# A background plan over 64 steps instead of 32, and experts added one by one instead of some in couples

## What is computed

```python
for i in range(DEPTH):                                    # 2 layers
    if i % 2 == 0: y = diff_attention(h)                  # paged K/V cache for the 8 new tokens
    else:          y = short_conv(h)                      # h @ w_in (3072 columns), width 3, @ w_out
    h = layer_norm(ALPHA * h + y)
    h = layer_norm(ALPHA * h + peer_ffn(h))
    h = h + sigmoid(h @ w_gate) * (p @ w_proj)

def peer_ffn(x):                                          # for each token
    q = (x @ w_q).reshape(8 heads, 2, 128)
    s = einsum(q, keys)                                   # 8 heads x 2 x 128 key scores
    sv, si = top_k(s, 16)
    cand = sv[0][:, None] + sv[1][None, :]                # 256 candidates of a head
    top_s, top_p = top_k(cand, 16)
    idx, g = expert ids, softmax(top_s)                   # 16 experts of a head, 128 of a token
    a = dot(x, u_tab[idx])                                # rows of 1024
    return sum(g * gelu(a) * v_tab[idx])                  # rows of 1024
```

## Time and profile before

| | us |
|---|---|
| median of three runs | 3244.95 |
| lowest and highest | 3240.28, 3246.25 |
| the profiled execution | 3244.58 |
| its span, first to last instruction | 3242.7 |
| TensorE busy (mean granted clock 0.975 of 2.4 GHz) | 2933.3 |
| VectorE, ScalarE, GpSimd busy | 2304.2, 1271.8, 1231.2 |
| first gather issued, last gather issued | 339.7, 3187.7 |

### The profile page before, as it was taken

The page is one execution under the profiler, slowest core; times in us unless marked ns, Lnnn a source line. Parts: engine busy times, 40 slices in busy tenths (PEclk is TensorE's granted clock), DMA queues, the critical chain, the costliest instruction groups (busy, mean ns, idle before and its releaser), DMA issues.

```text
span 3242.7 us, 33343 instructions
## 1 busy us (share of the span) xinstructions
PE 2933.3 (90%) x9278; PEld 1634.9 (50%) x9278; DVE 2304.2 (71%) x5838; ACT 1271.8 (39%) x3559; POOL 1231.2 (38%) x1100
## 2 busy tenths in 40 slices
PE   9998999989877989999898899999899887779998
PEld 7765555545533545555454355555455333334544
DVE  0654677777688788776767777778767888767754
ACT  0143333343334553333433463333334444345642
POOL 0100344444444444343334444334433454444441
PEclk9998999999999999999999999999999999999999
DMA  5514899999999999999899999999999999999996
GB/s 181 208 66 160 332 421 421 421 421 421 421 421 417 399 416 399 421 421 416 366 421 421 421 420 421 421 419 398 421 408 421 406 418 421 421 420 395 421 422 267
DMA packets 179256, 1242.82 MB, mean 383 GB/s; under 512 B 20038, under 2 KB 23366, under 8 KB 32640
## 3 DMA queue, kind: packets, MB, share of 16 engines
q0 software_dynamic: 156896, 1115.93, 83.4%
q1 hardware_dynamic: 22032, 123.73, 9.6%
q10 hardware_dynamic: 144, 1.05, 0.1%
HBM read 1234.16 MB, written 6.50 MB: 383 GB/s over the span
## 4 chain that ended last, share of the span: by engine, by line
PE 43%; DMA 33%; DVE 14%; ACT 4%; issue 2%; DVEq 2%; ACTq 1%; POOL 0%; SPq 0%; POOLq 0%
DMA arena<-in_uv,idx 32%; PE acc L1773 19%; DVE arena L1576 7%; PE bank L1799 6%; PE bank L1808 6%; PE bank L1631 3%; PE bank L1671 2%; PE acc L1782 2%; ACT diag L1164 1%; DVEq L1484 1%; ACT L1142 1%; ACT act_w L1151 1%; DMA arena<-in_uv,small 1%; PE bank L1676 1%; PE bank L1719 1%
## 5 line engine op out<-in xcount | busy, mean ns | idle before, releaser
L1773 PE MATMUL acc<-arena,diag 128*128 128x512 f32 x3864 | 1792.3, 611 | 236.0 <-ACT diag L1164 235.2
L993 POOL DMA_INDIRECT arena<-in_uv,idx x1024 | 1180.2, 1153 | 1646.7 <-PE acc L1773 1311.4
L1576 DVE CUSTOM_DVE_ANT_0 arena<-arena,h 128x1024 f32<-128x1024 f32 x1024 | 1227.6, 1221 | 452.8 <-DMA arena<-in_uv,idx 449.0
L1773 PEld LDWEIGHTS acc<-arena,diag 128*128 128x128 f32 x3864 | 731.2, 195 | 1156.6 <-issue 771.7
L1148 ACT ACTIVATE act_w<-dots 128x2 f32<-128x2 f32 x520 | 105.8, 203 | 1504.0 <-DVE dots L1576 1503.5
L1808 PE MATMUL bank<-hT,panel 128*128 128x264 f32 (+2 forms) x1792 | 405.4, 381 | 10.6 <-ACT hT L1115 6.6
L1808 PEld LDWEIGHTS bank<-hT,panel 128*128 128x128 f32 x1792 | 337.4, 191 | 103.0 <-issue 53.6
L1164 ACT ACTIVATE diag<-cst,act_w 128x128 f32<-128x128 f32 x966 | 336.4, 394 | 52.7 <-PE acc L1773 19.7
L1151 ACT ACTIVATE act_w<-act_w 128x1 f32<-128x1 f32 x1040 | 249.9, 287 | 43.0 <-issue 0.7
L1148 ACT ACT_TABLE_LOAD x127 | 162.9, 1283 | 1.8 <-issue 0.2
L1799 PE MATMUL bank<-panel,qT 128*128 128x256 f32 (+1 forms) x640 | 144.4, 379 | 0.0
(11 more groups left out here) (219 smaller groups left out, 2251.1 us busy)
## 6 DMA issues: line engine op xcount, KB each, us to landing
panel<-in_panels SPq DMA_DIRECT2D x95, 1024.0 KB, 9.1
arena<-in_uv,idx POOLq DMA_INDIRECT x1024, 20.0
arena<-in_cache_k POOLq DMA_DIRECT2D x16, 512.0 KB, 5.7
arena<-in_cache_v POOLq DMA_DIRECT2D x16, 512.0 KB, 5.0
arena<-in_panels SPq DMA_DIRECT2D x6, 1024.0 KB, 7.0
arena<-out_y_s POOLq DMA_DIRECT2D x8, 512.0 KB, 6.4
lng<-in_ln SPq DMA_DIRECT2D x6, 512.0 KB, 12.8
lnb<-in_ln SPq DMA_DIRECT2D x6, 512.0 KB, 16.1
```

The source lines that it names most:

```text
L993: nc.gpsimd.indirect_dma_start(uv[:, slot_of(e), :], None, uv_dram[layer], bass.IndirectOffsetOnAxis(ids[:, r:r + 1], 0)).then_inc(gathere ...
L1576: V.tensor_tensor_reduce(uv[:, slot_of(e), 0:D], uv[:, slot_of(e), 0:D], x_rows, 1.0, 0.0, ALU.mult, ALU.add, dots[:, G % 2, r:r + 1]).the ...
L1773: m = mm(acc[:, half * 512:(half + 1) * 512], diag[:, r % DIAGS, :], uv[:, slot_of(e), D + half * 512:D + (half + 1) * 512], start=False, ...
```

## The change

The plan has 64 steps a tile, one for each pair, and the halving of lots is gone. A piece behind a fence, or behind a change to `turn`, goes at least two steps on, and what is left of its lane is then spread by `COST` over what is left of the lane's room. Three lanes have other bounds, and the last normalization of blocks 0 and 1 (layer 1) is laid into steps 48 to 55 of tile (1,2), where it had stood at the end of (1,1) and the start of (1,2). No pair is joined: `joined_pairs`, `join_two`, `add_joined`, the estimates of load and the scaling of a row by ScalarE are taken out, and all 520 pairs go by `add_two`.

```diff
@@ window(layer, b, *lanes)
-            lots = [[] for _ in range(4 * HEADS if b < TB else 2)]
+            lots = [[] for _ in range(8 * HEADS if b < TB else 4)]
             for first, last, pieces in lanes:
-                total, so_far = sum(COST[x.kind] for x in pieces), 0
-                at, before = first, None
+                rest, so_far = sum(COST[x.kind] for x in pieces), 0
+                at, base, before = 2 * first, 2 * first, None
                 for x in pieces:
-                    if before and (x.fence or x.kind == "turn" and before != "turn" or before == "stage"):
-                        at = min(at + (2 if before == "norm_b" else 1), last - 1)
-                    at = max(at, first + int(so_far * (last - first) / total))
+                    if before and (x.fence or x.kind == "turn" and before != "turn"):
+                        at = min(at + 2, 2 * last - 1)
+                        base, rest, so_far = at, rest - so_far, 0
+                    at = max(at, base + int(so_far * (2 * last - base) / rest))
                     lots[at].append(x)
                     so_far += COST[x.kind]
                     before = x.kind
@@ build
-        window(0, 2, (3, 22, r3), (22, 32, rs[:13]), (0, 32, early))
+        window(0, 2, (2, 22, r3), (22, 32, rs[:13]), (0, 32, early))
...
-        tile0, tile1 = self.norm(3, (0,), True), self.norm(3, (1,), True)
-        window(1, 1, (0, 11, r1[17:]), (19, 32, r2[:25]), (0, 30, late), (30, 32, tile0))
+        norms = self.norm(3, (0,), True) + self.norm(3, (1,), True)
+        window(1, 1, (0, 11, r1[17:]), (19, 32, r2[:25]), (0, 30, late))
...
-        window(1, 2, (0, 4, r2[25:]), (4, 24, rs), (24, 25, side), (26, 27, spread), (25, 32, r3[:9]), (2, 6, tile1))
+        window(1, 2, (0, 4, r2[25:]), (4, 23, rs), (23, 24, side), (25, 26, spread), (27, 32, r3[:9]), (24, 28, norms))
@@ window_pairs
-    for t, lot in enumerate(lots):
-        cut = (len(lot) + 1) // 2
-        for half, part in enumerate((lot[:cut], lot[cut:])):
-            out.append((2 * t + half, first + t // 2, 2 * (t % 2) + half, t // 4, part))
-    return out
+    return [(t, first + t // 4, t % 4, t // 8, lot) for t, lot in enumerate(lots)]
@@ TensorE, for each pair
-                    if q > 0 and (G, q - 1) in plan.joined:
-                        add_joined(G, q - 1)
-                    elif q == 0 and (G - 1, 3) in plan.joined:
-                        add_joined(G - 1, 3)
-                    if (G, q) not in plan.joined:
-                        add_two(G, q)
+                    add_two(G, q)
```

More of the change, by code:

```diff
@@ L469, in build @@
         self.settle()
-        self.joined = {}
-        for kind, layer, b, lots in steps:
-            if kind == "window" and b < TB and layer + b > 0:
-                for t in joined_pairs(layer, b, lots):
-                    self.joined[first_group(layer, b) + t // 4, t % 4] = len(self.joined)
-        return steps
-    def turn_of_diag(self, e):
-        seen = e - DIAGS
-        while seen >= 0 and (seen // GROUP, seen % GROUP // 2) in self.joined:
-            seen -= DIAGS
-        return seen + 1
+        return steps
 def first_group(layer, b):
@@ L488, in first_group @@
     return layer * GROUPS + sum(HEADS * 2 if x < TB else 1 for x in before)
-def joined_pairs(layer, b, lots):
-    out, behind = [], 0
-    parts = [part for _, _, _, _, part in window_pairs(layer, b, lots)]
-    for t in range(1, len(parts) - 1):
-        part = parts[t]
-        behind += sum(map(tensor_load, part)) - PAIR_ROOM - 5 * sum(x.product and x.panel is not None and x.kind != "turn" for x in part)
-        behind = max(behind, 0)
-        near = sum(map(vector_load, parts[t])) + sum(map(vector_load, parts[t - 1]))
-        if behind > JOIN_GAIN and near <= JOIN_ROOM and (not out or out[-1] < t - 1):
-            out.append(t)
-            behind -= JOIN_GAIN
-    return out
 def window_pairs(layer, b, lots):
     first = first_group(layer, b)
-    out = []
-    for t, lot in enumerate(lots):
-        cut = (len(lot) + 1) // 2
-        for half, part in enumerate((lot[:cut], lot[cut:])):
-            out.append((2 * t + half, first + t // 2, 2 * (t % 2) + half, t // 4, part))
-    return out
+    return [(t, first + t // 4, t % 4, t // 8, lot) for t, lot in enumerate(lots)]
 DRAM_PANELS = [("qk", 0, 8), ("v", 0, 4)] + [(name, layer, count) for name, count in
@@ L807, in build @@
         gelu_done = sem("gelu_done")
-        weighted = sem("weights_on_diagonal_or_rows")
-        joined = sem("pairs_of_rows_summed")
+        diag_ready = sem("diag_ready")
         slot_done = sem("slots_done")
@@ L1770, in add_two @@
                     e = G * GROUP + r
-                    pe.wait_ge(weighted, e + 1)
+                    pe.wait_ge(diag_ready, e + 1)
                     for half in range(2):
@@ L1776, in add_two @@
                     m.then_inc(slot_done, 1)
-            def add_joined(G, q):
-                e = G * GROUP + 2 * q
-                pe.wait_ge(joined, plan.joined[G, q] + 1)
-                for half in range(2):
-                    m = mm(acc[:, half * 512:(half + 1) * 512], const("ident"),
-                           uv[:, slot_of(e), D + half * 512:D + (half + 1) * 512], start=False, stop=True,
-                           skip_group_check=True)
-                m.then_inc(slot_done, 2)
             def open_product(x):
```

35 lines of the change are left out of this document (3 added, 32 removed).

## The result

The changed kernel takes 3249.24 us in the median of 12 runs (3245.85 to 3254.91), the kernel before 3241.48 us in the median of the 12 beside them (3238.4 to 3246.25): 1.0022 of its time, 95% interval 1.0015 to 1.003. The prediction was 3229.3 us with a range up to 3247. The time went 8 us up where some 15 us down were expected.

The account below looks back on a forecast made before the run. The prediction took the kernel as bound by gather transfers, with gains only where these pause. From 3244.58 us it took 20.3 for regained pauses and added 5.0 for TensorE's overrun: 3229.3 us, 8-in-10 range 3221 to 3247.

Parts of the forecast that it names:

- Lost transfer time is a window's length times what its DMA share lacks to 1.: Seven pauses, at 1075 to 2955 us, priced by mean DMA share: together 22.3 us, of which 9.4 at 1585.
- all 20.3 us: Gain from moving pieces over 64 steps: all the pauses' lost time but the 2.0 us at 1075.
- Its bounds (9.4 to 22.3): Limits of the moved steps' gain: only the pause at 1585 us, 9.4, or every pause, 22.3 us.
- rival 1: Tiles (1,0) and (1,1): TensorE becomes the bound, its two stretches 22.6 and 5.7 us longer; 3257 us, chance 0.13.
- What is late next there is the next gather, so the 9.4 us come back whole.: Tile (0,3), pause at 1585: with TensorE's wait and lump of products gone, all 9.4 us are regained.
- The overrun, 5.0 us: From 1851.4 to 2323.1 TensorE falls 14.9 us behind without joined pairs; the ring absorbs 9.9, cost 5.0 us.
- Tile (0,0), "0, at most 2 us": Block 1's normalization in one step and transposes ahead of the pair delay gather 18; four gathers in flight cover it.
- Couples "worth 0": Removing 37 sums relieves VectorE and ScalarE, worth 0; TensorE's added 64 us is hidden where it has room.
- What would show it: Old pauses gone, TensorE at least 98% busy in (1,0) to (1,1), that stretch 470 to 480 us, earlier landings.
- the fourth sign: Second half of the stretch in (1,0) to (1,1): gathers land some 10 us after issue instead of 20.
- Rival 2: Pauses come from something else, such as VectorE's routing or TensorE's clock; only 5.4 us go: 3244 us, chance 0.20.
- The Trainium skill's rule on TensorE's load share: Stretch from 1851.4: weight loads busy 55%, so TensorE has room, the added work costs 0; sum 3224.3 us.

Follow-up runs that it names:

- half_add: The kernel before, with TensorE adding only columns 0 to 511 of the weighted rows, every gather still made: 3240.53 us, 0.9995 of before.
- only03: The kernel before with its couples, only tile (0,3) laid out over 64 steps and the keys' load five steps earlier: 3243.35 us, 1.0001 of before.
- t00_keys: The changed kernel, without couples, with tile (0,0) laid out as before and the load of the keys five steps earlier: 3244.4 us, 1.0002 of before.
- no_couples: The kernel before with its plan of 32 lots, but no pair joined: 3243.51 us, 1.0005 of before.
- tile00_old: The changed kernel with tile (0,0) alone laid out in 32 lots as before: 3244.19 us, 1.0003 of before.
- couples_64: The changed kernel with 32 couples put back by the old rule on the plan of 64 steps: 3250.24 us, 1.0024 of before.

## Why one part lags: tried, and left open

DMA queues of the page, kernel before (packets, MB, share of 16 engines):

```profile
q8 instruction: 74, 1.21, 0.2%
...
q14 instruction: 110, 0.90, 0.1%
```

The profile counts the fetches of instructions among the packets of the 16 DMA engines, 16 KB a packet in q8 and 8 KB in q14. The packets in q8 go up and down with TensorE's instructions, and those in q14 went up with SyncE's, as the runs below show. If all fetches for TensorE fell on one DMA engine, that could be the one behind. Three runs were made for it, besides `half_add`.

> The kernel before with 160 further instructions of SyncE behind each weight load (waits for a semaphore that is long set; some 15,000 in all), issued while SyncE is idle. They compute nothing and move nothing but themselves: nearly 1 MB of instructions, some 120 fetches of 8 KB at 0.32 us, 38 us if all fall on one DMA engine, 2.4 us if they are spread over sixteen. Theory F with fetches as the reason why one DMA engine is behind: the lag grows faster and the time rises by 20 to 40 us, 3263 to 3283, with every compute engine as busy as before. Rival (the lag has another reason, or these fetches fall on another DMA engine): 3243 to 3248.

Measured: 3243.01 us, 1.0002 (0.9992 to 1.0011). The edit is `for _ in range(160): sp.wait_ge(s_zero, 1)` behind each panel load; q14 went up from 110 packets to 171, half of what I had expected, 20 us at 0.32 us each if they all fell on the engine behind. The time did not move, but the landings did. Over gathers 160 to 240, 68 of them complete in this trace, the 16th part stays at 21.3 us in the mean (21.4 before), the 14th at 14.1 (14.0), and the 15th goes from 14.5 to 18.2. Over 600 to 640 it is much the same (15.7 to 19.7, 24 gathers complete), over 880 to 940 it is gone. One further part has fallen behind, which suggests that SyncE's fetches fall on one DMA engine, and not on the slowest.

> The kernel before with 24 further instructions of TensorE ahead of each pair's additions in tiles (0,1) and (1,2) (waits for a semaphore that is long set, 3072 in all, 0.2 MB), where TensorE idles for 48 and 63 us. Theory F with TensorE's fetches: 12 more fetches of 16 KB, 8 to 13 us slower, 3251 to 3256, TensorE's busy time unchanged. Theory G: 3243 to 3246.

Measured: 3244.24 us, 1.0001 (0.9992 to 1.0011), q8 with 80 packets. The edit: `for _ in range(24): pe.wait_ge(s_hT[0], 16)` ahead of each pair in two tiles. Against `half_add` with 59 packets there are 21 more, at 1.06 us each in the trace 22 us; the medians stand 3.7 us apart. Twenty-two would have shown, and over gathers 200 to 250 the last part lands after 20.1 us in this kernel and 20.7 in `half_add`. So TensorE's fetches are not what keeps that engine behind.

> The kernel before with 193 couples instead of 37: every second pair of which VectorE has the room is joined, whether TensorE is behind or not, the opposite of the change. 156 pairs with two matmuls less each on TensorE. Theory F with TensorE's fetches: 5 fetches of 16 KB less, 4 to 6 us faster, 3237 to 3239, if the waits for joined rows stay hidden. Theory G: 3242 to 3246. Theory B (couples are worth something of themselves, TensorE's time): 10 us or more.

Measured: 3260.33 us, 1.0052 (1.0038 to 1.0065). The edit takes `behind > JOIN_GAIN` out of the rule. All three theories missed. The waits of this kernel (in total, times, longest), where joined rows now hold TensorE up:

```profile
PE acc L1782 <- DVE arena L1584: 393.2, 127, 8.1
```

and its windows of tiles (0,1) and (1,2):

```profile
710.00:1066.00 356.00, 272.91 (x706) 140.81 (x704) 299.90 (x766) 146.88 (x375) 145.02 (x129) 0.88 1.00 407
2545.00:2877.00 332.00, 229.19 (x454) 94.23 (x454) 298.86 (x748) 142.78 (x360) 160.99 (x128) 0.83 0.97 397
```

12 and 19 us of transfers are lost in them by the rate, and the lag of the last part is down to 0.5 us over gathers 840 to 880 (10.4 against 9.9 us). By theory F the cover is used up, and the rest of the pauses is paid.

What makes one part lag stays open. It is not TensorE's work, nor its instructions, nor the ones added to SyncE. The instructions of VectorE, ScalarE and GpSimd were not varied, nor the weight loads, nor the way in which the gathers are issued; nor was it tested whether one DMA engine is slower than the others in full flow by itself (alone, in the pause, it kept its share of the rate). The traces kept here do not tell which DMA engine a packet ran on. The lag grows steadily while nothing pauses, from 0.7 us over gathers 40 to 80 to 7.4 over 200 to 240. No complete version was found that beats the kernel before. If theory F holds, none can that only fills pauses shorter than the lag.

## Why the prediction was wrong, step by step

- **"Lost transfer time is a window's length times what its DMA share lacks to 1."** This is the step that failed, and all 20.3 us hang on it. The pauses went as predicted, in the earlier trace rows and in the windows after. They were worth nothing that can be measured: `only03` takes the largest away and stands at 1.0001, and `t00_keys`, without any of them and without the loss of tile (0,0), at 1.0002 (0.9993 to 1.0011). The mean share counts the fifteen DMA engines that had got ahead; the last part of a gather decides when its rows can be used, and in the pause at 1585 its engine lost some 3 us and not 9.4. Its bounds (9.4 to 22.3) were drawn within the same measure and so could not hold the measured value, 0. (The upper end of the sum's range counts 16.8 us back at the places outside the two stretches; by the prediction's own figures it is 15.8, as in rival 1, and the end 3241.)
- **"What is late next there is the next gather, so the 9.4 us come back whole."** The next gather was issued earlier indeed (`only03`: gather 452 by 12 us, beyond its lead of 3.0). But behind the place the last part lands 22.1 us after issue in the changed kernel, instead of 21.2, although the other parts land 10 us sooner.
- **The overrun, 5.0 us.** In its own stretch it was right in kind: TensorE was busy for 476.9 us (484.1 predicted), and the stretch was 478.0 us long, 6.3 more than before, where 5.0 less the 2.5 of its pause, 2.5 more, were predicted. As a price of the whole it was nothing that shows (`no_couples`): that kernel's tile (1,0) took 365.5 us instead of 361.9, and its (1,1) 360.5 instead of 363.8.
- **Tile (0,0), "0, at most 2 us".** This term of the sum was mis-sized, by 6 to 8 us, and it decided the sign. The norm pieces and the transposes ahead of the pair were named there, but "four gathers are still in flight" was no cover, since TensorE's wait of 2.8 us and two transposes came on top; and the panel of the query product at 437 was not looked at, though the lump of four products that the change took apart is what released its home early.
- **The gap behind `stage`** was in the diff and in no step. It made the longest new wait (8.96 us). Taking it away gained nothing (`t00_keys` against `tile00_old`, 1.0002 and 1.0003), by the same cover that made the gains worthless.
- **Couples "worth 0" where TensorE has room**: right, and beyond the places for which it was said (`no_couples` at 1.0005, `couples_64` at 1.0024 beside 1.0022 without).
- **"What would show it"** named the pauses gone, TensorE at 98% and more, the stretch in 470 to 480 us. All three came true beside a wrong time. They were signs of the pauses and not of the time. Of the fourth sign, landings at 10 us in the second half of the stretch, the 15 parts show it (10.1) and the 16th doesn't (16.2).
- **The rivals.** Rival 2, "the pauses come from something else", gave 3244. That it lies nearest to the measured time is luck: the pauses did come from where the prediction had them, and went. None held that a real pause can be free. The Trainium skill's rule on TensorE's load share (Perfetto Trace Analysis, Identifying the Most-Contended Engine), weighed there, has the load share read in place of the busy time. In the stretch the trace sided with the busy time (6.3 us longer at 99.8% busy, weight loads 57%). For the whole kernel `half_add` sides with the rule: at 90% busy and a load share of 50% TensorE had room.

## What to carry to other kernels

Before a pause of the DMA engines is booked as lost time, look at when the parts of one transfer land. Where one part lagged by more than the pause was long, filling the pause gained nothing here; what has to be found then is why that engine is behind. A cheap test comes ahead of any rewrite: make the same pause on purpose at that place and see whether the time rises by its length, or take half of the suspected engine's work away. And when a layout rule is changed for a whole program, walk the places where the buffers have only just started to fill. Here that was tile (0,0), and there two waits of 2.8 and 5.0 us made the whole loss.

## What the runs showed that I had not expected

One of the sixteen parts of a gather landed 10 us behind the other fifteen for most of the program, at a mean DMA share of 1.01, and the lag vanished in a pause (from 10.4 us to 0.9), in which that one engine went on alone at 16 to 33 GB/s. Extra instructions on an idle SyncE, 61 fetches, moved a second part from 14.5 to 18.2 us over gathers 160 to 240, and the time not at all. And TensorE could lose 531 of its 2933 us of work, or be busy for 320 us without a gap, with no change in the kernel's time in either case.
